# Two gated feed-forward stages: two pairs of chunks each by seven block products in place of eight

## The reference

```
D_MODEL = 1024
SEQ = 256
D_FF = 2816

def swiglu(x, w_gu, w_down):
    gate, up = jnp.split(x @ w_gu, 2, axis=-1)
    return (jax.nn.silu(gate) * up) @ w_down
...
h = h + 0.5 * swiglu(rmsnorm(h, ffn1_norm[l]), ffn1_w_gu[l], ffn1_w_down[l])
...
h = h + 0.5 * swiglu(rmsnorm(h, ffn2_norm[l]), ffn2_w_gu[l], ffn2_w_down[l])
```

## Time and profile before

| what | value |
| --- | --- |
| median of 3 runs | 990.17 us (990.16 to 990.27) |
| the profiled execution | 990.05 us |
| its span, first to last instruction | 988.0 us |
| PE busy | 981.1 us, 99% |
| DVE busy | 705.7 us, 71% |
| ACT busy | 597.4 us, 60% |
| transfer queue q1 (all loads and transposes of SP) | 201.21 MB, 64.3% of 16 engines |

### The profile page before, as it was taken

The page is one execution under the profiler, slowest core; times in us unless marked ns, Lnnn a source line. Parts: engine busy times, 40 slices in busy tenths (PEclk is TensorE's granted clock), DMA queues, the critical chain, the costliest instruction groups (busy, mean ns, idle before and its releaser), DMA issues.

```text
span 988.0 us, 12498 instructions
## 1 busy us (share of the span) xinstructions
PE 981.1 (99%) x4576; PEld 805.1 (81%) x4576; DVE 705.7 (71%) x998; ACT 597.4 (60%) x809; POOL 120.7 (12%) x109
## 2 busy tenths in 40 slices
PE   8999999999999999999999999999999999999998
PEld 6788888888777788888888888888888888888887
DVE  5756565668987667665656677876689878977685
ACT  7344444577666636434444576868876548977772
POOL 0000000022300000000000031249923001000000
PEclk9999999999999999999999999999999999999999
DMA  8987776586544536657575578667665664695542
GB/s 261 284 264 263 229 257 215 170 310 194 167 129 157 184 128 219 214 174 249 170 249 173 188 224 245 176 192 173 217 227 188 238 214 150 201 315 176 188 111 95
DMA packets 167577, 201.96 MB, mean 204 GB/s; under 512 B 58081, under 2 KB 113770, under 8 KB 167402
## 3 DMA queue, kind: packets, MB, share of 16 engines
q1 hardware_dynamic: 166938, 201.21, 64.3%
q10 hardware_dynamic: 592, 0.14, 0.1%
HBM read 182.45 MB, written 5.77 MB: 190 GB/s over the span
## 4 chain that ended last, share of the span: by engine, by line
PE 96%; DVE 2%; ACT 1%; DMA 1%; issue 0%; POOL 0%; SPq 0%; ACTq 0%; DVEq 0%
PE bank L2380 23%; PE bank L2382 23%; PE bank L2381 23%; PE bank L2483 4%; PE bank L2482 4%; PE bank L2481 4%; PE bank L2602 3%; PE bank L2603 3%; PE bank L2601 3%; PE bank L2395 1%; PE bank L2637 1%; PE bank L2752 1%; DMA raw<-in_ffn_w_gu 1%; DVE lo L1626 0%; PE bank L2652 0%
## 5 line engine op out<-in xcount | busy, mean ns | idle before, releaser
L2380 PE MATMUL bank<-hi,xh 128*128 128x512 f32 (+1 forms) x904 | 359.1, 397 | 1.4 <-DVE lo L1981 1.3
L2382 PE MATMUL bank<-hi,xl 128*128 128x512 f32 (+1 forms) x904 | 351.6, 389 | 0.0
L2381 PE MATMUL bank<-lo,xh 128*128 128x512 f32 (+1 forms) x904 | 351.0, 388 | 0.0
L1609 DVE TENSOR_TENSOR lo<-raw,hi 128x2048 fp32r<-128x2048 f32 (+1 forms) x82 | 187.4, 2287 | 94.7 <-ACT hi L983 94.7
L983 ACT ACTIVATE hi<-raw 128x2048 fp32r<-128x2048 f32 (+1 forms) x85 | 161.1, 1898 | 90.9 <-PE bank L2483 57.4
L2380 PEld LDWEIGHTS bank<-hi,xh 128*128 128x128 f32 x904 | 169.8, 188 | 38.7 <-issue 2.1
L2382 PEld LDWEIGHTS bank<-hi,xl 128*128 128x128 f32 x904 | 169.7, 188 | 35.6
L2381 PEld LDWEIGHTS bank<-lo,xh 128*128 128x128 f32 x904 | 170.0, 188 | 32.8
L1626 DVE TENSOR_TENSOR lo<-raw,hi 128x1024 fp32r<-128x1024 f32 (+1 forms) x108 | 131.6, 1228 | 42.6 <-ACT hi L992 41.9
L992 ACT ACTIVATE hi<-raw 128x1024 fp32r<-128x1024 f32 x102 | 104.5, 1051 | 8.9 <-PE bank L2382 8.9
L2481 PE MATMUL bank<-hi,hh 128*128 128x512 f32 x176 | 69.1, 392 | 0.0
(11 more groups left out here) (303 smaller groups left out, 1341.7 us busy)
## 6 DMA issues: line engine op xcount, KB each, us to landing
raw<-in_w_in SPq DMA_DIRECT2D x48, 1024.0 KB
raw<-in_ffn_w_gu SPq DMA_DIRECT2D x82, 512.0 KB
raw<-in_ffn_w_down SPq DMA_DIRECT2D x22, 1024.0 KB
raw<-in_w_down SPq DMA_DIRECT2D x16, 1024.0 KB
raw<-in_w_out SPq DMA_DIRECT2D x8, 1024.0 KB
operand<-in_w_up SPq DMA_DIRECT2D x8, 1024.0 KB, 7.2
raw<-in_w_up SPq DMA_DIRECT2D x8, 1024.0 KB
distance_table<-ftab SPq DMA_DIRECT2D x8, 576.0 KB
```

Of the source, the lines that this page charges most:

```text
L1609: nc.vector.tensor_tensor(lo[s][:, :, 0:width], raw[s][:, :, 0:width], hi[s][:, :, 0:width].bitcast(F32), ALU.subtract).then_inc(lo_done, 1)
L2380: nc.tensor.matmul(o, sh, wh, start=first and j == 0, stop=False, skip_group_check=onto)
L2381: nc.tensor.matmul(o, sh, wl, start=False, stop=False, skip_group_check=onto)
L2382: ins = nc.tensor.matmul(o, sl, wh, start=False, stop=last and j == 3, skip_group_check=onto)
```

## The change

Chunks 4 and 5, and 8 and 9, of each gated stage become pairs (`FIRST_PAIRS`), each by seven block products. The other seven chunks stay plain. In the pair the down units of the two chunks before stand third and fifth of nine units:

```
+FIRST_PAIRS = ((4, 8), (4, 8))
+PAIRS = (2, 6)
+OPERAND = {"p1": 0, "p2": 1, "p6": 5, "p7": 2, "p5": 4, "p4": 1, "p3": 3}
+
+def gated_order(pairs):
+
+    order = [("u", i, u) for i in range(2) for u in range(2)]
+    for i in range(2, NF1 - 1, 2):
+        d = [("d", i - 2 + c, 0) for c in range(2)]
+        if i in pairs:
+            p = {k: (k, i, 0) for k in OPERAND}
+            order += [p["p1"], p["p2"], d[0], p["p6"], d[1], p["p7"], p["p5"], p["p4"], p["p3"]]
+        else:
+            order += [("u", i, 0), ("u", i, 1), d[0], ("u", i + 1, 0), ("u", i + 1, 1), d[1]]
+    i = NF1 - 1
+    return order + [("u", i, 0), ("u", i, 1), ("d", i - 2, 0), ("d", i - 1, 0), ("d", i, 0)]
```

The order on ACT and DVE through a pair (`n` is the pair's first unit; DVE's is the second):

```
+            def gated_pair(f, j):
+
+                i = PAIR_AT[j][1]
+                n = pair_unit(j, "p1")
+                split_hi(n + 2)
+                keep(j, 0)
+                split_hi(n + 3)
+                split_hi(n + 4)
+                ffn_hi(f, i - 1)
+                ffn_act(f, i, 0)
+                split_hi(n + 5)
+                keep(j, 1)
+                split_hi(n + 6)
+                ffn_planes(f, i, 0)
+                split_hi(n + 7)
+                keep(j, 2)
+                split_hi(n + 8)
+                split_hi(n + 9)
+                ffn_act(f, i, 1)
+                split_hi(n + 10)
+                ffn_planes(f, i, 1)
+                split_hi(n + 11)
+                ffn_act(f, i + 1, 1)
+                ffn_act(f, i + 1, 0)
+                split_hi(n + 12)
+                ffn_hi(f, i)
...
+            def gated_pair(f, j):
+
+                i = PAIR_AT[j][1]
+                n = pair_unit(j, "p1")
+                weight_sum(j, 3)
+                split_lo(n + 2)
+                if j % 2 == 1:
+                    ffn_lo(f, i - 2)
+                split_lo(n + 3)
+                ffn_merge(f, i - 1)
+                add_product(j, 0)
+                split_lo(n + 4)
+                ffn_lo(f, i - 1)
+                ffn_hidden(f, i, 0)
+                split_lo(n + 5)
+                weight_sum(j, 4)
+                split_lo(n + 6)
+                split_lo(n + 7)
+                split_lo(n + 8)
+                add_product(j, 1)
+                split_lo(n + 9)
+                split_lo(n + 10)
+                ffn_hidden(f, i, 1)
+                add_product(j, 2)
+                split_lo(n + 11)
+                ffn_hidden(f, i + 1, 1)
+                ffn_hidden(f, i + 1, 0)
+                ffn_merge(f, i)
+                split_lo(n + 12)
+                ffn_lo(f, i)
```

And PE's waits for a free bank before an up unit:

```
                     for t in range(NT):
-                        if u == 0:
-                            pe.wait_ge(f.hidden, 2 * f.past + 2 * i + t - 1)
-                        ins = portion(n + u, t, G[t], xh, xl, 4 * u, u == 0, u == 1)
+                        if u == 0 and i > 1:
+
+                            if i - 2 in f.plain:
+                                pe.wait_ge(f.hidden, 2 * f.past + f.order(i - 2, t))
+                            elif i % 2 == 0 and t == 0:
+                                pe.wait_ge(f.hidden, 2 * f.past + f.order(i - 2, 1))
+                            elif i % 2 == 0:
+                                pe.wait_ge(pairs.added, 3 * f.pair(i - 2) + 1)
+                            elif t == 0:
+                                pe.wait_ge(pairs.added, 3 * f.pair(i - 2) + 3)
+                        ins = portion(n, t, (G, X)[i % 2][t], xh, xl, 4 * u, u == 0, u == 1)
```

More of the change, by code:

```diff
@@ L85 @@
 C_ROWS = C_NORM + 4 * KT
-PAIRS = (2, 6)
 def last_order():
@@ L243, with __init__ @@
 class GatedFfn(Ffn):
-    def __init__(self, sem, name, base, norm, earlier=None):
-        super().__init__(sem, name, base, NF1, norm)
-        self.past = 0 if earlier is None else NF1
+    def __init__(self, sem, name, stage, norm, earlier=None):
+        super().__init__(sem, name, (U_F1, U_F2)[stage], NF1, norm)
+        self.stage, self.pairs = stage, FIRST_PAIRS[stage]
+        self.past = stage * NF1
+        self.plain = [i for i in range(NF1) if i // 2 * 2 not in self.pairs]
+        self.g0_past = 0 if earlier is None else len(earlier.plain)
         if earlier is None:
@@ L255, in __init__, with unit, second, order @@
             self.hh, self.hl, self.d_part = earlier.hh, earlier.hl, earlier.d_part
[L257 to L262, removed]
+    def unit(self, kind, i, b=0):
+        return self.base + GATED[self.stage].index((kind, i, b))
+    def second(self, i):
+        return i % 2 == 1 and i - 1 in self.pairs
+    def order(self, i, t):
+        return 2 * i + (1 - t if self.second(i) else t) + 1
+    def pair(self, i):
+        return PAIR_AT.index((self.stage, i // 2 * 2))
+    def in_pair(self, i):
+        return i not in self.plain
 class SquaredFfn(Ffn):
@@ new lines, in keep @@
+            def keep(j, k):
+                act.wait_ge(used, pair_unit(j, ("p1", "p6", "p7")[k]) + 1)
+                stage, i = PAIR_AT[j]
+                if k == 0 and i == (FIRST_PAIRS + (PAIRS,))[stage][0]:
+                    act.wait_ge(pairs.s_lo, 4 * stage + 4)
+                elif k == 0 and stage < 2:
+                    act.wait_ge(ffns[stage].hidden, 2 * ffns[stage].past + ffns[stage].order(i - 1, 1))
+                nc.scalar.activation((c11, c12, c22)[k], G[0][:, :], ACT.Copy).then_inc(pairs.kept, 1)
@@ L1076, in ffn @@
             def ffn(f, width=lambda n: W):
-                ffn_act(f, 0, 0, f.base + 1)
+                n = f.base
+                one, two = (PAIR_AT.index((f.stage, i)) for i in f.pairs)
+                ffn_act(f, 0, 0)
                 if f.base == 0:
                     half_squares(3)
-                split_hi(f.base + 3)
-                ffn_act(f, 0, 1, f.base + 1)
-                split_hi(f.base + 4)
-                with act.Fori(1, f.chunks - 1) as i:
-                    ffn_iter(f, i, f.base + 2, i - 1)
@@ L1800, in x_sums @@
                         (x_block[4], x_block[4], x_block[2], ALU.add))):
+                    if not first <= count < past:
+                        continue
+                    stage = 2 if f is last else f.stage
                     if count > 0:
[L1802 to L1807 removed]
+                        dve.wait_ge(pairs.s_made, 5 * stage + count)
@@ L2542, in product @@
                     if i - 2 in PAIRS:
-                        pe.wait_ge(last.added, 3 * j - 2)
+                        pe.wait_ge(pairs.added, 3 * j - 2)
                     else:
```

1004 lines of the change are left out of this document (590 added, 414 removed).

## The result

The changed kernel takes **995.6 us** (four executions: 994.25, 994.8, 996.4 and 996.59) against 990.2 us before: ratio 1.0053, 95% interval 1.0036 to 1.0071. It is slower by 5.4 us, where the forecast was slower by 2.5. The profiled execution is the fastest of the four.

A forecast was written before the change was run, and what follows sets the result against it. PE's row of matmuls was taken as the bound in the gated stages. Saving -10.9, pair exits +10.5, stage ends +2.6, small covers +0.3 summed to +2.5 us, giving 992.7 us as the median; range 989.8 to 997.

The forecast's parts named there:

- worked-out forecast: Whole kernel: the terms summed to 992.7 us, with a band of 991.5 to 994 us at chance 0.50.
- rival 3: First stage: the transfer queue becomes a bound, three hl late by 1 to 2 us, 995 to 998 us; chance 0.15.
- signs of being wrong: Exit waits under 1.5 us or over 3.5, stage ends that cost nothing, or PE waiting for a load.
- signs of holding: Four PE waits of about 2.4 us behind pairs, two of about 1.3 before a down unit, DVE nearly never idle, clock 1.00.
- The reading of what bounds the kernel: Gated feed-forward stages: a row of matmuls on PE hides all other engines, so only PE's matmuls and waits cost time.
- The saving: Four pairs in the gated stages: 48 matmuls fewer at 0.2268 us each, 10.9 us less.
- Term 1: Exit of each pair: PE waits for DVE's hidden step behind a low part, 2.62 us at four pairs, +10.5 us.
- Term 2: Each stage's end: chunk 8's down unit waits for hl, held up through the next down unit's load, 1.32 us twice, +2.6.
- The small covers: hl of chunk 0 behind four differences and hl of the pair's first chunk with little to spare: +0.3 us (0 to 2).
- Rival 1: Stage ends: load and copy come early, so the stage-end waits vanish, 990.1 us, no difference; chance 0.20.
- Rival 2: Pair exits: bank 0 comes free early, no exit wait, faster at 982.2 us; chance 0.10.
- Rival 4: Four pair exits: idle PE brings the clock down, a product at half rate each, 10.9 us more, 1003.6 us; chance 0.03.

The follow-up runs named there:

- e11: e6 with three hl steps earlier on DVE and, behind every pair, hh and hl of the next chunk ahead of a load-bound unit's parts: 979.98 us.
- e1: Changed kernel with the DVE hidden step that reads bank 0 ahead of the second up unit's low part, in all four pairs: 985.9 us.
- e12: e11 with the e1 edit undone, so the hidden step stands again behind the second low part in all four pairs: 994.44 us.
- after_again: The changed kernel once more, no edit, for a second profile: 993.88 us, one execution.
- e2a: Changed kernel with the e1 move in the first pair of each stage only: 990.28 us.
- e2b: Changed kernel with the e1 move in the second pair of each stage only: 992.17 us.
- e3: Changed kernel with nine extra matmuls into an idle bank behind p3 of each pair, keeping PE busy in the exit wait: 994.14 us.
- e13: e11 with the stage-end edit of e5 undone, behind the second pair of each stage: 984.7 us.
- e5: e1 plus, behind each stage's second pair, hh and hl of chunk 8 ahead of the high and low parts of chunk 9's down unit: 985.31 us.
- e6: e5 plus, on ACT, the high part of p3's weights ahead of the third saved copy of bank 0: 983.73 us.
- e9: e3 (exit waits kept, PE kept busy in them) plus the stage-end order of e5: 993.36 us.

## Why the prediction was right or wrong

**The number** was in part luck. The measured 995.6 us lies in the range (989.8 to 997), but outside the band of the worked-out forecast (991.5 to 994, chance 0.50), at a time that the prediction gave to rival 3 (995 to 998 us), whose three late `hl` of the first stage neither profile of the changed kernel has. In the first profile one of its own signs of being wrong is met, the stage ends cost nothing, and one of its signs of holding is missing, the clock of 1.00. The direction and the mechanism of the two main terms held.

**The reading of what bounds the kernel** held. But for small distances and the start (both below), every microsecond lost was a wait of PE or a slower clock of PE; the some 60 us of work that DVE and ACT got each (the earlier trace rows and the page above) cost next to nothing in e11.

**The saving** of 10.9 us held: e11 keeps 10.2 of it.

**Term 1** held in mechanism and size. 2.32 us at the exit, 0.11 behind it, 0.19 and some 0.08 at p3: 2.7 per pair where 2.62 was forecast, 10.8 us for 10.5. From T to the exit it is 5.57 to 5.58 us at all eight exits of the two profiles, 5.57 in the sum, and e1 and e12 show the cause: DVE's order.

**Term 2** held in mechanism, was 0.9 us short, and in the first profile its waits can't be seen at all. With the clock kept up it cost 3.55 us in `after_again` and 3.49 in e1, where 2.6 was the forecast. In `after_again` the first of the two waits came as forecast (1.27 against 1.32), the second at 2.28, and there the load took 6.47 us from its issue where the sum has 5.28, by one row of another stage. Two links of the chain have a spread. At the stage ends of the seven profiles that keep this order (both of the changed kernel, e1, e2a, e2b, e3, e13) the load took 5.1 to 6.5 us, and the step from the transpose's issue to the load's, 1.29 in the sum, took 1.25 to 2.64: at e2a's second stage end, with a wait of 2.32 us, the load was quick (5.13) and this step was the late one. I took a single value for each.

**The small covers** (0.3, 0 to 2) cost nothing in both profiles of the changed kernel, and more in others. The wait of chunk 0's `hl` behind the four differences was 0 in these two, 1.11 us in e3 and 1.69 in e5. The one of chunk 4 at 106 us, 0.17 to 1.42 us in five profiles, is the `hl` of the pair's first chunk, which the prediction gave 0.3 us to spare; it is Term 2's pattern in the first pair, and a late load takes more than that from it. From e6 to e11, which took these two and chunk 9's away, the median fell by 3.75 us; in e6's profile the three waits of this kind sum to 3.4.

**Rivals 1 to 3.** Rival 1's condition, stage ends that cost nothing, held in the first profile, but for a reason that the prediction had not: the fallen clock, and not a quick load. Rival 2 is out: all exits of the changed kernel wait 2.3 us. Rival 3's late `hl` in the first stage are missing from both profiles of the changed kernel; waits of its kind came up in profiles of the edited kernels, 0.2 to 1.7 us, at 106 us and at 43 us, where nothing has been edited yet, so the changed kernel's unprofiled executions may have had them too.

**Rival 4, the clock**, had a chance of 0.03 and a price of 2.7 us at each of four exits. It does happen, at a lower price (1.6 us) and not each time. In the first profile it makes 3.2 of the 4.4 us of longer span, and Term 2 is zero; in `after_again` it is the reverse. That idle time of PE brings it is what e3 and e9 show: with matmuls put into the exit waits, 14 of 16 executions kept a mean clock of 1.00, of the changed kernel's one of five. The step that failed is the evidence I took against it: the 0.87 us of the earlier trace rows are the part of one wait that lies in that window, 1.1 us in all by the last row, and say nothing of one of 2.3 us. I had no row of a longer wait in dense work and should have given this rival far more. The Trainium skill (TensorE: Matmul & The Clock Gate, "HAM oscillation — how this bites in real kernels") warned of waits between groups of matmuls that bring PE back to the lower clock; the traces agree that it happens, with two differences. The waits of its example are longer (3 to 5 us), while here the seven falls stand behind waits of 2.0 to 2.6 us, and most waits of this length bring nothing.

**The sum.** For the first profile: -10.9 + 10.8 + 3.2 (clock) + 0.5 (a later start: the same point is passed at 27.4 against 26.9 us, and at 26.0 to 27.0 in the eleven edited kernels, whose start is the same) = +3.6; its last matmul is 4.3 us later than that of the kernel before. For `after_again`: -10.9 + 10.8 + 3.55 + 0.2 (behind those two waits) - 0.3 (start) = +3.4, measured 3.97 in the same way. In both 0.6 to 0.7 us lie in distances of under 0.12 us that I assigned to nothing. The median is another 1.35 us above the first profile. Which waits the unprofiled executions had isn't recorded. The clock isn't enough for it: the execution of 996.4 us has the mean clock of the profiled one (0.997) and took 2.15 us more. Their mean clocks (0.995 to 0.998) and e11's narrow spread point to both causes together, and their shares stay open.

## What to carry to other kernels

When one engine is full, saving work on it is won or lost on the order of its suppliers: follow, for every bank and every operand it waits for, what stands ahead of the releasing instruction on that engine's queue, and move steps of half a microsecond ahead of those of two. Here a loss of 0.5% became a gain of 1.0% by seven moves in the order of ACT and DVE and nothing else, six of this kind and one, in e6, that puts a high part ahead of a short copy. After one such wait is removed, expect the next to appear behind it: judge a repair by the waits that are left, and by the spread of the runs, not by the time alone, since two costs can hide one another (a slow clock made PE late and so hid a late operand). For a chain with a transfer in it, carry the spread of the transfer's rows through the sum, and look for the same pattern at every place where the order repeats.

## What the runs showed of the hardware

- A wait of PE of about 2 us and more was followed in some cases by a granted clock of 0.50 (1.2 of 2.4 GHz). In all profiles of this study the gated stages have 22 waits in which 1.9 us or more were lost, counted by the distance of the starts less the usual 0.23 (16 exits, 6 before a down unit), and 7 falls, each behind one of them; there is none behind the shorter ones (0.7 to 1.8 us). Every fall came 1.0 to 1.4 us after PE had resumed, lasted 3.4 us and cost 1.6. The same program showed two falls in one execution and none in the next. What decides between them stays open.
- After a wait the first matmul is followed by the second at 0.31 us, not 0.23, at every exit, and the ones behind it run slightly apart; a wait costs 0.11 us more than its length.
- The time from the issue of a 1 MB load behind a transpose to the start of its high part was 5.1 to 6.5 us at thirteen stage ends of seven profiles (at a fourteenth the high part waited for PE), and SP issued it 1.25 to 2.64 us behind the transpose. The wait before the down unit of chunk 0, at 43 us, was 0 to 1.7 us with the same order.
